# Twelve of 22 feed-forward up steps as seven half-block products, in a two-layer hybrid kernel

## What is computed

```python
def conv_ffn(h, w_up, conv_w, conv_b, w_down):     # w_up 1024 x 5632, w_down 2816 x 1024
    u = h @ w_up
    up = jnp.pad(u, ((0, 0), (CONV_W - 1, 0), (0, 0)))          # CONV_W = 3, along the tokens
    u = conv_b + sum(conv_w[j] * up[:, j:j + S] for j in range(CONV_W))
    gate, val = jnp.split(u, 2, axis=-1)
    return (jax.nn.silu(gate) * val) @ w_down
```

## Time and profile before

| | |
|---|---|
| three executions | 1191.27, 1191.84 (median), 1192.90 us |
| profiled execution | 1191.57 us, of which its span 1189.8 us |
| TensorE busy | 1174.8 us, 99% of the span |
| VectorE, ScalarE, GpSimd busy | 73%, 52%, 29% |
| up steps 1 to 10 of layer 0 / layer 1 | 316.0 to 533.8 / 852.6 to 1070.4 us |
| down units of layer 0 / layer 1 | 533.8 to about 645 / 1070.4 to about 1183 us |

### The profile page before, as it was taken

How to read it: one execution, slowest core, us unless ns; L and a number is a source line. 1 busy time by engine, 2 the same in 40 slices (tenths; PEclk the granted TensorE clock), 3 DMA queues, 4 the chain that set the end, 5 groups by cost and what they waited for, 6 DMA issues and landing times.

```text
span 1189.8 us, 18961 instructions
## 1 busy us (share of the span) xinstructions
PE 1174.8 (99%) x6874; PEld 999.6 (84%) x6874; DVE 862.7 (73%) x1502; ACT 617.0 (52%) x1033; POOL 348.5 (29%) x429
## 2 busy tenths in 40 slices
PE   9999999999999999999999999999999999999998
PEld 7768886778888888888999887988888888888998
DVE  6588968945766566579897898855766666579986
ACT  6554337855434333345565789945534334335563
POOL 0633547830042522211000366730042421211000
PEclk9999999999999999999999999999999999999999
DMA  7555352253398785436554110053387574326553
GB/s 281 182 187 199 142 202 65 73 142 106 106 238 238 199 217 184 175 109 211 186 160 138 62 37 2 1 125 107 106 192 179 156 172 130 106 71 208 176 173 127
DMA packets 51555, 174.54 MB, mean 147 GB/s; under 512 B 4720, under 2 KB 6128, under 8 KB 41504
## 3 DMA queue, kind: packets, MB, share of 16 engines
q1 hardware_dynamic: 36352, 127.51, 31.3%
q0 software_dynamic: 15136, 46.14, 16.3%
HBM read 171.50 MB, written 52.47 MB: 188 GB/s over the span
## 4 chain that ended last, share of the span: by engine, by line
PE 93%; DVE 3%; ACT 2%; issue 1%; POOL 0%; DVEq 0%; ACTq 0%; POOLq 0%
PE ps L2554 28%; PE ps L2556 27%; PE ps L2555 27%; PE ps L2269 3%; PE ps L2253 3%; PE ps L2069 1%; PE ps L2520 1%; PE ps L2110 1%; PE ps L2237 1%; PE ps L2140 1%; ACT probs L977 1%; DVE w_lo L1705 1%; DVE xT L1725 0%; PE ps L2121 0%; ACT w_hi L1148 0%
## 5 line engine op out<-in xcount | busy, mean ns | idle before, releaser
L2554 PE MATMUL ps<-h_hi,w_hi 128*128 128x512 f32 x704 | 274.4, 390 | 0.0
L2555 PE MATMUL ps<-h_lo,w_hi 128*128 128x512 f32 x704 | 273.9, 389 | 0.0
L2556 PE MATMUL ps<-h_hi,w_lo 128*128 128x512 f32 x704 | 273.9, 389 | 0.0
L1394 DVE TENSOR_TENSOR w_lo<-raw,w_hi 128x2048 fp32r<-128x2048 f32 (+1 forms) x62 | 123.0, 1984 | 118.3 <-ACT w_hi L887 118.3
L1216 ACT ACTIVATE cv<-u_in,vec 128x512 f32<-128x512 f32 x88 | 71.2, 816 | 180.4 <-DVE u_in L1835 178.3
L887 ACT ACTIVATE w_hi<-raw 128x2048 fp32r<-128x2048 f32 (+1 forms) x72 | 121.8, 1692 | 69.1 <-PE ps L2556 69.1
L2554 PEld LDWEIGHTS ps<-h_hi,w_hi 128*128 128x128 f32 x704 | 132.2, 188 | 27.6 <-issue 0.7
L2556 PEld LDWEIGHTS ps<-h_hi,w_lo 128*128 128x128 f32 x704 | 132.2, 188 | 27.6
L2555 PEld LDWEIGHTS ps<-h_lo,w_hi 128*128 128x128 f32 x704 | 132.2, 188 | 27.3
L762 POOL TENSOR_TENSOR v<-act 128x256 f32<-128x256 f32 x16 | 43.3, 2707 | 345.2 <-DVE act L1872 345.2
L2554 PE MATMUL ps<-a_hi,w_hi 128*128 128x256 f32 (+1 forms) x440 | 138.9, 316 | 2.2 <-DVE a_lo L1709 2.2
(11 more groups left out here) (276 smaller groups left out, 2421.6 us busy)
## 6 DMA issues: line engine op xcount, KB each, us to landing
raw<-in_f_up SPq DMA_DIRECT2D x44, 1024.0 KB, 5.0
w_sums<-in_f_w_down POOLq DMA_DIRECT2D x22, 1024.0 KB, 8.7
w_sums<-in_f_w_down POOLq DMA_DIRECT2D x44, 512.0 KB, 9.0
raw<-w_sums SPq DMA_DIRECT2D x44, 512.0 KB, 4.2
raw<-in_a_in_wide SPq DMA_DIRECT2D x12, 1024.0 KB, 6.1
raw<-in_f_w_down SPq DMA_DIRECT2D x22, 512.0 KB, 3.9
raw<-in_f_w_down SPq DMA_DIRECT2D x22, 256.0 KB, 4.0
bias_tiles<-bias_rows SPq DMA_DIRECT2D x1, 4096.0 KB, 27.0
```

The lines of the kernel that those rows point to most:

```text
L1394: dve.tensor_tensor(w_lo[:, s, 0:n], raw[:, s, 0:n], w_hi[:, s, 0:n].bitcast(F32), ALU.subtract)\
L2554: pe.matmul(dst, s_hi, m_hi, start=start, stop=False)
L2555: pe.matmul(dst, s_hi, m_lo, start=False, stop=False)
L2556: return pe.matmul(dst, s_lo, m_hi, start=False, stop=stop)
```

## The change

`SEVENS` names the up steps in the new form: 5 to 8 in layer 0, 1 to 8 in layer 1. In such a step the 256 gate and 256 value channels, the two halves of the 1024 features and the two halves of the tokens form 2 x 2 blocks, and seven products of half blocks (each 2 parts x 4 k x 3 matmuls of 256 columns) take the place of eight. Four of the seven need sums of feature halves (`sums_of_features`, once a layer, from `gained_features`), four need sums of weights, made in HBM like those of the down part (`w_two`, `w_more`: a copy, then accumulating DMAs). Outside the seven steps, weight units become quarters (128 x 1024) in four slots; a seven step takes seven of them. All loops of the up steps are unrolled.

The products, on TensorE:

```diff
+SEVENS = ((5, 6, 7, 8), (1, 2, 3, 4, 5, 6, 7, 8))
...
+                    for j, (b, moving) in enumerate(((0, 0), (2, 3), (0, 4), (1, 1), (0, 5), (2, 2), (0, 6))):
...
+                        pe.wait_ge(w_lo_done, U_UP[l] + 2 + m + 1)
...
+                        if j in (2, 4, 5, 6):
+                            pe.wait_ge(f_snap, LANDED + SNAP_AT[l][i] + {2: 1, 4: 3, 5: 2, 6: 4}[j])
+                        for part in range(2):
+                            for k in range(4):
```

The step on ScalarE:

```diff
+                    m, behind = unit_of(l, i), i - 1 in SEVENS[l] or i == 1
+                    if behind:
+                        tap2(i - 1, 2)
+                        tap2(i - 1, 3)
+                    keep(i, 0)
+                    unit_hi(l, m + 4)
+                    if behind:
+                        silu(i - 1)
+                    keep(i, 1)
+                    unit_hi(l, m + 5)
+                    keep(i, 2)
+                    unit_hi(l, m + 6)
+                    unit_hi(l, m + 7)
+                    keep(i, 4)
+                    unit_hi(l, m + 8)
+                    unit_hi(l, m + 9)
+                    tap2(i, 0)
+                    tap2(i, 1)
+                    unit_hi(l, m + 10)
```

The step on VectorE:

```diff
+                    if i - 1 in SEVENS[l]:
+                        second_row(i - 1)
+                        unit_lo(l, m + 3)
+                    if behind and i > 1:
+                        taps(i - 1, (0, 1))
+                    unit_lo(l, m + 4)
+                    if behind:
+                        if i == 1:
+                            taps(0, (0, 1))
+                        else:
+                            taps(i - 1, (2, 3))
+                    unit_lo(l, m + 5)
+                    if i == 1:
+                        taps(0, (2, 3))
+                        sum_lo(l, 3)
+                    first_row(i, 0)
+                    if behind:
+                        gated(i - 1)
+                    unit_lo(l, m + 6)
+                    second_row_sum(i)
+                    unit_lo(l, m + 7)
+                    unit_lo(l, m + 8)
+                    first_row(i, 1)
+                    unit_lo(l, m + 9)
```

In the last step VectorE's splits of down unit 1, the `third` of unit 2, and the first part of unit 2 move ahead of the last taps or of gate*value:

```diff
+                    taps(i, (0, 1))
+                    if last:
+                        third(l, 1)
+                    scaled(i, 2)
+                    scaled(i, 3)
+                    if last:
+                        seven_lo(l, 1, 0)
+                        seven_lo(l, 1, 1)
+                        third(l, 2)
...
                     taps(i, (2, 3))
+                    if last:
+                        seven_lo(l, 2, 0)
+                    gated(i)
```

More of the change, by code:

```diff
@@ L99 @@
 G_COLS = 36
+SEVENS = ((5, 6, 7, 8), (1, 2, 3, 4, 5, 6, 7, 8))
 U_A = 0
 U_AOUT = U_A + 16
+N_UP = [2 + sum(7 if i in SEVENS[l] else 4 for i in range(1, UP_STEPS)) for l in range(2)]
 U_UP = [U_AOUT + KD, 0]
-U_DOWN = [U_UP[0] + 2 * UP_STEPS, 0]
+U_DOWN = [U_UP[0] + N_UP[0], 0]
 U_B = U_DOWN[0] + FT
@@ L1236, in step, with tail, keep @@
                         sc.activation(cv[:, q, :], cv[:, q, :], ACT.Silu).then_inc(f_silu, 1)
-                    tap2(i, 2, first)
-                    tap2(i, 3, first)
-                    if last:
+                def tail(i):
+                    tap2(i, 2)
+                    tap2(i, 3)
+                    silu(i)
+                def keep(i, j):
+                    x, _, v_bank = seven_banks(l, i)
+                    bank, dst = {0: (x, kept[:, 0].rearrange("p (a n) -> p a n", a=2)),
+                                 1: (v_bank, kept[:, 1].rearrange("p (a n) -> p a n", a=2)),
+                                 2: (x, u_in[:, 0:2, 2 + HS:2 + S]), 4: (x, u_in[:, 2:4, 2 + HS:2 + S])}[j]
+                    z = SEVENS[l].index(i)
+                    sc.wait_ge(f_done, DONE_AT[l][i] + j + 1)
+                    if j < 2 and z:
+                        sc.wait_ge(f_in, IN_AT[l][i - 1] + j + 1)
+                    if j >= 2:
+                        sc.wait_ge(f_t0, 2 * FT * l + 4 * (i - 1) + j)
+                    sc.activation(dst, both(ps[:, bank, :]), ACT.Copy).then_inc(f_snap, 1)
@@ new lines, in plain_step @@
+                def plain_step(i):
+                    m = unit_of(l, i) if i else -4
+                    first, last = SEVENS[l][0], i == UP_STEPS - 1
+                    if i - 1 in SEVENS[l]:
[4 more added lines that the diff above has]
+                        gated(i - 1)
+                    scaled(i, 0)
+                    if i == first - 1 and i:
+                        for j in range(4):
+                            sum_lo(l, j)
+                    scaled(i, 1)
+                    if i == 0 and first == 1:
+                        unit_lo(l, 2)
+                        unit_lo(l, 3)
+                        sum_lo(l, 2)
+                        scaled(0, 2)
+                        scaled(0, 3)
+                        return
+                    if last:
@@ L1882, in _ @@
+                unit_lo(l, 0)
+                unit_lo(l, 1)
+                if SEVENS[l][0] == 1:
+                    sum_lo(l, 1)
+                chain.then_wait(dve.memset(u_in[:, :, 0:2], 0.0))
+                dve.wait_ge(rbc_ok, l + 1)
+                for i in range(UP_STEPS):
+                    if i in SEVENS[l]:
+                        seven_step(i)
+                    else:
+                        plain_step(i)
             first_attention()
```

476 lines of the change are left out of this document (370 added, 106 removed).

## The result

The changed kernel takes 1198.45 us (median of 6 runs, 1195.31 to 1201.48), the kernel before 1191.63 (6 runs, 1191.1 to 1192.9): a ratio of 1.0056, interval 1.0043 to 1.0069. The forecast was 1180. The profiled execution took 1198.06 us with a span of 1196.2, against 1191.57 and 1189.8 before.

A forecast was written before the change was run, and what follows sets the result against it. TensorE, busy 1174.8 of 1189.8 us, was taken as the bound. The terms summed as 1191.57 - 19.2 - 5.0 + 8.1 + 2.4 + 2.0 = 1179.9, predicted as 1180 us, with a range of 1168 to 1189.

The forecast's parts named there:

- Part 1: Products of the up steps: a seven step takes 20.16 us instead of 21.76, saving 19.2 us over twelve.
- Rival (d): Seven steps' 256-column matmuls go slower, say 0.127 us, so steps are no shorter: +19, 1199 us; chance 0.04.
- Part 2: Entries of the down units: waits for VectorE's low parts go, 5.4 us less 0.4 in layer 0, saving 5.0.
- Part 3: VectorE and ScalarE in a seven step: 18.7 and 13.4 us of work fit in 20.16 us, cost zero.
- Part 6: DMA queues: 19.8 of 20.16 us full in seven steps, 2 us lost; first and second attention unpriced, latter up to 4.
- Part 4: Layer 1, step 0 to its first seven step: new TensorE waits of 3.8, 1.8, 1.6 and 0.8 us, together 8.1.
- Part 5: Layer 0, step 4 to 5: keep(5, 0) ends late, one wait of 2.4 us, between 0 and 3.
- Rival (b): Ten seven steps with sums: loads fall behind at 42% of their rate, +53, 1231 us; chance 0.08.
- rival (c): Milder (b), VectorE 8 to 10% slower, or normed late in second attention: 5 to 10 us more, 1185 to 1190; chance 0.18.

The follow-up runs named there:

- second_only: Changed kernel with seven steps in layer 1 alone, their weight sums issued where queues have room, copies by SyncE: 1183.33 us, 0.9926 of the kernel before.
- no_weight_sums: Changed kernel without the DMAs that copy and sum up weights, quarters loaded from f_up itself, output not the reference's: 1184.11 us, 0.9935 of the kernel before.
- entry_reordered: second_only with kept and the fourth quarter ahead of step 0's last two taps, and VectorE's taps earlier, in layer 1's step 1: 1177.78 us, ratio 0.9885.

## Why the prediction was wrong, step by step

**Part 1, right.** 20.06 us a step against 20.16. By the gap that the Trainium skill gives ("TensorE: Matmul & The Clock Gate", section "Back-to-back issue gap"), which that page calls the one of a single matmul by itself, it would have been 18.3 (the text has 18.4); the rows decided, as they did in the forecast. Rival (d), whose 1199 is the number nearest to the measurement, hit it by luck: its steps no shorter than before are refuted by 20.06 us against 21.76. Nor does its own working hold: 0.127 us a matmul make a step of 21.3 us, which saves 0.4.

**Part 2, right in layer 1, wrong in layer 0.** 2.2 of 2.7 us came in layer 1; in layer 0 nothing did, where 2.3 were expected. The text feared the landing of the last sum; it landed after 6.6 us. What was late was VectorE: its first low part for unit 1 starts 4.5 us into the down units, in layer 1 1.9 us into them. The step that failed: the gate sums were counted only as delay of GpSimd's next DMA issue, not as a load on VectorE beside them. With them spread out (second_only) the four units take 23.6 us, the forecast's whole gain.

**Part 3, right.** 18.8 and 13.3 us of work in a step, and steps that close at 20.06. One step (4 of layer 1) lost 2.1 us to a quarter for which ScalarE had waited 4.1 us; that is Part 6. Without the copies and sums of the up weights (no_weight_sums) ScalarE still waits 3.6 us there and TensorE 1.5, so what is left to explain it are the step's own loads and the sums of down weights.

**Part 4, right.** 8.1 us forecast (its terms add up to 8.0). The waits were 3.3, 1.5, 1.4 and 0.4 us; steps 1 and 2 are 7.8 us longer than two undisturbed ones. That entry_reordered takes 4.3 to 4.7 us off the seven steps by the order alone shows the mechanism.

**Part 5, too small.** Steps 5 and 6 of layer 0 are 3.8 us longer than two undisturbed ones, forecast 2.4: the wait for `kept` came twice, 2.3 and 1.1 us.

**Part 6, the step that failed.** It priced the queues inside the seven steps, where they cost little, and put everything outside them at nothing. The copies of the first attention, which it laid out by bandwidth, cost nothing that shows. But it had no line for the eight sums `w_two` of layer 0 beside the projection and the first loads of the up steps: 1.85 us of waiting and 1.7 of clock. It allowed the second attention up to 4 us and took 0: 3.0. And it had no line for the 16 sums between the down units of layer 0, the largest loss of all: 5.2 us in this profile, up to 11.6 in others. The prediction's own rule, that a moved step's DMAs count at each queue and place, was kept in one part and dropped in another. Rival (b) had the right mechanism, a load that lands late beside sums, at the wrong place and with 1231 us far too dear; the "`normed` late in the second attention" of rival (c) came, as one of several losses. The down units' loads were not wanted sooner than the quarters of the seven steps: the five late ones were wanted 6.4 to 12.0 us after their issue, where the text has 6 to 9 us for a quarter. They landed later: after up to 14.1 us, against 5.1 at most in the kernel before and 10.7 at most for a quarter. Why the queues serve them worse at much the same share stays open.

**What no part had: the clock.** Each wait was priced at its length. Behind the first stage the changed kernel has eleven stops of TensorE of 0.9 us and more where the one before has five, and some of them are followed by a spell of the lower clock: 1.7 us at step 0 and 1.7 us more than before in the mixer, in the profiled execution, the latter chance as said above. Its runs spread over 6.2 us, those before over 1.8. The clock is a part of that and not all: an estimate of what it took in each of the six, one minus the mean granted clock times the span, is 6.0 to 12.0 us, and the spans without it still lie between 1186.2 and 1190.2. The down units of layer 0, 93.0 to 99.4 us in four profiled executions, are another part. Against its own profiled execution the forecast is 18.2 us short: 5.2 + 3.0 for the two stretches, 4.3 for the start and steps 0 to 4, 2.6 for layer 0's down entry, 2.4 at the mixer, 1.1 + 0.8 + 0.5 + 0.1 for savings that came out smaller, less the 2.0 that Part 6 had, 18.0.

The range was too narrow for the same reason: its cases for the queues, (b) and (c), had their price inside the seven steps, or as one allowance of 5 to 10 us, and none added several stages up.

## What to carry to other kernels

When a change makes new weights by DMA, list every stage in which one of its transfers is in flight, with the DMA share there, the time between issue and use of that stage's own loads and how late they may land; a share of 0.9 was free in plain up steps and cost 5 to 12 us in down units. Price a new wait of a busy TensorE above its length, and look at the places where the form changes before the steady state: a few instructions in another order there gave 4.3 to 4.7 us, about what three seven steps save. Before a difference of 2 us in one stretch is explained, look at the same stretch in a second execution. If part of a change needs resources that the rest doesn't, try it without that part: seven steps in layer 1 alone, with their sums moved, are 15 us faster than the changed kernel, and 21 us with the reordered entry.

## What the runs showed of the hardware

- In the 14 profiled executions, that of before included, each spell of the lower clock within the kernel began between 1.4 us before and 2.1 us after TensorE resumed from a stop of at least 1.4 us (the last 20 us of the program left out). It lasted 3.4 or 6.8 us and cost half of that. Behind stops of 2.8 us and more it came in 19 of 24 cases, behind those of 2.1 to 2.6 us in 6 of 12, behind those of 1.4 to 2.0 us in 7 of 34, behind the 32 of 0.9 to 1.3 us in none. So whether a given stop is followed by one differs from execution to execution, and such stops widen a kernel's spread.
- Six stops of 3.42 us cost 30.1 us in their stretch, 5.0 each; six of 1.24 us cost 9.1, 1.5 each.
- Two taps of VectorE, 128x512 each, took 1.41 us alone and up to 2.46 beside tensor operations of GpSimd.
- A software DMA issued by GpSimd between its own operations took 0.6 to 1.1 us of its time; 11 of them issued by SyncE instead made the second attention 2.2 us shorter, with the same bytes moved.
- Beside 16 accumulating DMAs of 512 KB, loads of 256 and 512 KB for the down units landed after up to 14.1 us, without them after at most 5.1.
